# Four allocations of a float32 encoder trunk moved to different starts modulo 512 bytes

## The reference

```python
def swiglu(x, w_gate, w_up, w_down):
    return (jax.nn.silu(x @ w_gate) * (x @ w_up)) @ w_down

for l in range(DEPTH):
    g = norm_gains[l]
    h = h + 0.5 * rms_norm(swiglu(rms_norm(h, g[0]), ffn1_gate[l], ffn1_up[l], ffn1_down[l]), g[1])
    m = hybrid_mixer(rms_norm(h, g[2]), w_in[l], ..., w_out[l], cos, sin)
    h = h + rms_norm(m, g[3])
    h = h + 0.5 * rms_norm(swiglu(rms_norm(h, g[4]), ffn2_gate[l], ffn2_up[l], ffn2_down[l]), g[5])
```

## Time and profile before

| | us |
|---|---|
| median of 3 runs | 1955.1 |
| lowest and highest | 1944.96, 1957.04 |
| span of the profiled execution | 1954.7 |
| TensorE matmul busy | 1917.7 (98%) |
| VectorE busy | 1123.9 (57%) |
| ScalarE busy | 875.2 (45%) |
| GpSimd busy | 223.1 (11%) |

### The profile page before, as it was taken

One profiled execution on the slowest core, in us unless ns is written; L12 is line 12 of the kernel. 1 busy time (PEld: TensorE's weight loads), 2 busy tenths in 40 slices (PEclk: granted clock), 3 DMA queues, 4 the chain that ended last, 5 costly groups with the idle time before them and its releaser, 6 DMA issues.

```text
span 1954.7 us, 25496 instructions
## 1 busy us (share of the span) xinstructions
PE 1917.7 (98%) x9136; PEld 1546.1 (79%) x9136; DVE 1123.9 (57%) x1605; ACT 875.2 (45%) x1390; POOL 223.1 (11%) x433
## 2 busy tenths in 40 slices
PE   8999999999999999999999999999998999999998
PEld 7788888877667788888878888887875778888887
DVE  5775553287657655553277755434876576555423
ACT  4554432255654544432255444322666455444321
POOL 2841000023100000000058010000131000000000
PEclk9999999999989999999999999999998999999999
DMA  6334343342213333343333433433412123333331
GB/s 178 104 105 127 97 119 89 83 143 80 55 44 87 97 97 97 96 119 89 94 95 97 137 92 107 116 90 101 152 33 65 54 78 98 102 90 108 114 89 43
DMA packets 330956, 188.56 MB, mean 96 GB/s; under 512 B 6996, under 2 KB 325432, under 8 KB 329848
## 3 DMA queue, kind: packets, MB, share of 16 engines
q1 hardware_dynamic: 324008, 168.13, 29.8%
q0 software_dynamic: 5824, 18.79, 3.4%
q10 hardware_dynamic: 1040, 0.52, 0.1%
HBM read 175.72 MB, written 11.67 MB: 96 GB/s over the span
## 4 chain that ended last, share of the span: by engine, by line
PE 88%; DVE 4%; ACT 4%; issue 2%; DMA 1%; POOL 0%; DVEq 0%; ACTq 0%; POOLq 0%
PE ps L561 17%; PE ps L563 16%; PE ps L562 16%; PE ps L697 8%; PE ps L698 8%; PE ps L696 8%; PE ps L589 2%; PE ps L590 2%; PE ps L594 2%; PE ps L907 1%; ACT wh L1045 1%; PE ps L884 1%; PE ps L865 1%; DVE wl L1504 1%; ACT sig L1142 1%
## 5 line engine op out<-in xcount | busy, mean ns | idle before, releaser
L1504 DVE TENSOR_TENSOR wl<-raw,wh 128x1024 fp32r<-128x1024 f32 (+1 forms) x270 | 358.0, 1327 | 530.4 <-ACT wh L1045 529.1
L561 PE MATMUL ps<-xh,wh 128*128 128x512 f32 x1552 | 612.6, 395 | 5.6 <-DVE wl L1504 4.3
L563 PE MATMUL ps<-xh,wl 128*128 128x512 f32 x1552 | 606.2, 391 | 0.0
L562 PE MATMUL ps<-xl,wh 128*128 128x512 f32 x1552 | 605.9, 390 | 0.0
L1045 ACT ACTIVATE wh<-raw 128x1024 fp32r<-128x1024 f32 (+1 forms) x270 | 305.0, 1130 | 441.6 <-PE ps L698 331.4
L561 PEld LDWEIGHTS ps<-xh,wh 128*128 128x128 f32 x1552 | 292.6, 189 | 75.5 <-DVE wl L1504 9.3
L563 PEld LDWEIGHTS ps<-xh,wl 128*128 128x128 f32 x1552 | 292.3, 188 | 61.8
L562 PEld LDWEIGHTS ps<-xl,wh 128*128 128x128 f32 x1552 | 292.7, 189 | 59.1
L696 PE MATMUL ps<-Hh,wh 128*128 128x512 f32 x704 | 274.0, 389 | 0.0
L698 PE MATMUL ps<-Hh,wl 128*128 128x512 f32 x704 | 273.9, 389 | 0.0
L697 PE MATMUL ps<-Hl,wh 128*128 128x512 f32 x704 | 273.9, 389 | 0.0
(11 more groups left out here) (326 smaller groups left out, 2039.9 us busy)
## 6 DMA issues: line engine op xcount, KB each, us to landing
raw<-in_ffn_up SPq DMA_DIRECT2D x88, 512.0 KB, 3.8
raw<-in_ffn_down SPq DMA_DIRECT2D x64, 704.0 KB, 4.6
raw<-in_ffn_gate SPq DMA_DIRECT2D x87, 512.0 KB, 3.8
raw<-in_w_in SPq DMA_DIRECT2D x28, 512.0 KB, 4.1
raw<-in_w_out SPq DMA_DIRECT2D x16, 512.0 KB, 4.0
xrow<-in_x SPq DMA_DIRECT2D x2, 1024.0 KB, 8.6
ssm_t<-evict POOLq DMA_DIRECT2D x8, 256.0 KB, 3.1
ssm_v<-evict POOLq DMA_DIRECT2D x8, 256.0 KB, 2.7
```

The costliest lines, as they stand in the source:

```text
L561: pe.matmul(bank, w_tile(True, slot, kw), xh[:, kx, :], start=first, stop=False)
L562: pe.matmul(bank, w_tile(True, slot, kw), xl[:, kx, :], start=False, stop=False)
L563: return pe.matmul(bank, w_tile(False, slot, kw), xh[:, kx, :], start=False, stop=last)
L1504: V.tensor_tensor(w_low(slot, k0, nk), raw[:, slot4, 0:nk - k0, :], w_high(slot, k0, nk).bitcast(F32), ALU.subtract).then_inc(w_split, 1)
```

## The change

Three unused tensors are allocated: 64 bytes for each partition ahead of `xh`, 64 ahead of `wh` and 128 ahead of `wl`. Nothing reads or writes them. No instruction is added, removed or moved; only addresses differ.

```diff
         xl = sb("xl", [P, KD, SEQ], F32R)
+        sb("pad_xh", [P, 16])
         with ExitStack() as alias:
             yF = alias.enter_context(nc.sbuf_tensor("yF", [P, KD, SEQ], F32))
         xh = sb("xh", [P, KD, SEQ], F32R)
         raw = sb("raw", [P, RAW_SLOTS, KH, P])
+        sb("pad_wh", [P, 16])
         wh = sb("wh", [P, SPLIT_SLOTS, KH, P], F32R)
+        sb("pad_wl", [P, 32])
         wl = sb("wl", [P, SPLIT_SLOTS, KH, P], F32R)
```

## The result

The changed kernel takes 2003.8 us (median of 4 runs, 1999.7 to 2004.4) against 1954.6 us before (4 runs): a ratio of 1.0266, 95% interval 1.0242 to 1.0291. It is slower by 49 us. The profiled execution of the changed kernel has a span of 2002.6 us, 47.9 us over the 1954.7 us of before.

The account below looks back on a forecast made before the run. The prediction took 7440 float32r matmuls at 0.2267 us as the bound. Its terms for matmul stream, splits and DMAs were all 0, leaving the 1954.7 us span; forecast 1954 us, range 1916 to 1990 us.

Parts of the forecast that it names:

- What bounds the kernel: Whole kernel: 7440 float32r matmuls of 512 columns at 0.2267 us make 1687 us, 86% of the 1954.7 us span.
- first step: Float32r matmul stream: unlike operand starts change nothing, 0 us, with ends of 76 us either way.
- geometric argument: Matmul stream: weight load and running columns drift about 490 bytes, meeting nearly every relative place once wherever they start; 0 ns.
- float32 pair: Plain float32 matmuls, line 602 with unlike starts and line 944 with equal ones: both 0.43 us, so equal starts cost nothing there.
- slower rival: Lines 561 to 563, 696, 697: equal starts were the good case; 69 us more, or half; slower cases together 0.14.
- Steps two and three: Weight splits on VectorE and ScalarE, and DMAs into raw: new places cost 0 us, hidden under the matmuls.
- faster rival: Float32r matmuls: 10.2 ns each was a load and column conflict that goes; 1886 us, or 1917 for half; chance 0.16.
- drift argument: Matmul stream: load and columns drift about 490 bytes, so other starts move their meeting, not the number of meetings; 0 ns.

Follow-up runs that it names:

- micro1: Program without the kernel's trunk: only float32r matmul streams, 256 pairs of weight and column starts in 32-byte steps, plus patterns of three; 226.7 to 234.1 ns for each matmul.
- micro2: Program of matmul streams alone: 4-byte steps, mixed places, narrower loads, fewer columns, other types; unlike 4-byte steps 229.7 to 235.1 ns except 120 bytes, as good as equality.
- e5_all: Kernel before plus 64 unused bytes ahead of everything, all large tensors at 192 modulo 512 instead of 128; 1953.2 us, ratio 1.0010.
- e4_256: Kernel before plus the change's three unused tensors at the same places in the code, but 256 bytes each; 1948.6 us, ratio 0.9988.
- e3_wl: Kernel before plus only the 128 unused bytes ahead of wl, so wl and the feed-forward inside start at 256; 1988.7 us, ratio 1.0195.

## Why the prediction was wrong

- **What bounds the kernel** was right: 7440 float32r matmuls at 0.2267 us, 1 ns of which is 7.4 us. The measured 49 us are 6.6 ns for each of them on the average.
- **The first step failed**, in the geometric argument: the term for the matmul stream stood at 0 ns and measured 6.6 ns. I let the load and the column stream drift against each other by about 490 bytes and concluded that they meet every relative place once, wherever they start. micro1 refutes it with nothing but these streams: 226.7 to 234.1 ns by the start alone. The argument assumed that two steady readers lose time only where they meet; no row had shown that. The places repeat every 256 bytes, so 512 was also the wrong circle. The sign that I had given for a failure of this step, starts 0.230 us and more apart, is what the changed profile shows.
- **The float32 pair** of lines 602 and 944 was read rightly and was worth nothing. micro2 has 0.4292 us at all four differences that it tried. The pair held the type fixed at one that doesn't feel the place. I had written that a conflict could hide there and still used the pair against the slower rival.
- **Steps two and three**, price 0 for the splits and the DMAs, were right: 1234 and 1052 ns, landings longer by 0.1 us and hidden. By an estimate from the beats of the Trainium skill's page "DMA: Bandwidth & Descriptors", section "How a descriptor splits into AXI transactions", `raw` would have needed 10% more if the rule held for the SBUF side. The trace doesn't bear that out: e5_all, with `raw` at the same 192, has 3.9 us against 3.8, 3% more, and no loss of time that shows.
- **The slower rival, with 0.14, named the cause.** Equal starts are the good case. It was right on the place and on the direction. That the columns catch the load a second time, its picture of how, no run shows. Its term was mis-sized: 10.2 ns for 6736 matmuls and 2024 us, or half of it and 1989 us, where 6.6 ns for all 7440 came out. It took line 698 for exempt, since `Hh` and `wl` still agree at 384. The lines before and after it load the unlike `wh`, and its distance rose to 235 ns.
- **The faster rival** needed a place better than equality. Neither the 256 pairs nor the 32 fine steps have one: nothing lies under 226.6 ns. No start that was tried takes away any of the 11 ns over a bfloat16 matmul.
- **The range** ended at 1990 us because the slower case's full price lay beyond it. My two ends for an unseen price were even, -10.2 and +10.2 ns, but the drift argument had given the middle nearly all of the chance.

No version beats the kernel before: e4_256 and e5_all are level with it within their intervals.

## What to carry to other kernels

In a stream of float32r matmuls of 128 x 128 weights and 512 columns, let the weights and the columns start at the same place modulo 256 bytes, in every product that is dense; check the start addresses whenever a small tensor is added ahead of them, since 64 unused bytes cost this kernel 1.5%. The distance between the starts of neighbouring matmuls shows it at once: 0.227 us when they agree, mostly 0.229 to 0.241 us when they don't. Narrower loads and 256 columns were tried at one unlike place only, and it cost nothing there. An argument that an effect must average out is no row; where one nanosecond counts 7440 times, an unseen price should keep its chance until something of the same type has shown it.

## What the hardware showed that I had not expected

- The place of weights against columns matters in float32r (226.7 to 234.1 ns for 512 columns), with a period of 256 bytes, and at the four differences tried not in bfloat16 (215.8 ns) or plain float32 (429.2 ns for a record). The effect needs no other engine: micro1 has it with all of them idle.
- The price carries over to the neighbours. One unlike load in three costs at two matmuls (e3_wl), the same cycle of two streams can settle at 226.8 or 236.5 ns (micro2), and the order of `xh` with `wl` and then `xh` with `wh` at places 192, 384 and 256 reaches 241 ns, 7 ns over anything in the table of constant pairs.
- The Trainium skill's page "TensorE: Matmul & The Clock Gate", section "Step-by-step: what each phase is for", says of the two read ports that loading the next weights takes no bandwidth from the running matmul. For bfloat16 the runs agree (215.8 ns at four differences). For float32r the running stream isn't left untouched: where the load starts changes the distance by up to 7.4 ns. Whether that is bandwidth at these ports no run here shows.
- Open is what inside TensorE or its memory makes the period of 256, why a difference of 64 in one direction is cheap (228.9 ns) and in the other not (233.4), why narrower loads are dearer (230.3 ns for 64 columns against 226.7), and what decides which of its distances a mixed stream settles at. For these the runs give the prices, not the reason.
